# Latent heads' softmax weights turned by VectorE and moved through DRAM, and the ends of the first and last layer reordered

## What is computed

```python
for l in range(DEPTH_2):                       # 2 layers
    h = rmsnorm_2(x, pre_norm_g[l])
    z = h @ w_in[l]
    q_lat, kv_lat, k_pe, gb, gc, xin, q_mem, gate = split_cols(z)
    q = (rmsnorm_2(q_lat, q_norm_g[l]) @ w_uq[l]).reshape(b, s, MLA_HEADS, QK_HEAD_DIM)
    ...
    a_out = mla_attention(q, k, v)             # softmax(q k / sqrt(192)) v, per head
    c_out = short_gated_conv(gb, gc, xin, conv_w[l])
    ...
    m_out = memory_attention(q_mem.reshape(b, s, MEM_HEADS, MEM_HEAD_DIM), mem_n, w_mk[l], w_mv[l])
    y = jnp.concatenate([a_out, c_out, m_out], axis=-1) * jax.nn.silu(gate)
    o = y @ w_o[l]
    x = x + rmsnorm_2(o, post_norm_g[l])
```

## Time and profile before

| | us |
|---|---|
| median of 3 runs | 2250.86 |
| lowest and highest | 2250.55, 2252.74 |
| the profiled execution | 2250.03 |
| its span in the trace | 2248.2 |
| PE busy | 2224.8 (99%) |
| DVE busy | 1309.1 (58%) |
| ACT busy | 808.5 (36%) |

### The profile page before, as it was taken

One profiled execution on the slowest core, in us unless ns is written; L12 is line 12 of the kernel. 1 busy time (PEld: TensorE's weight loads), 2 busy tenths in 40 slices (PEclk: granted clock), 3 DMA queues, 4 the chain that ended last, 5 costly groups with the idle time before them and its releaser, 6 DMA issues.

```text
span 2248.2 us, 27822 instructions
## 1 busy us (share of the span) xinstructions
PE 2224.8 (99%) x10604; PEld 1851.7 (82%) x10604; DVE 1309.1 (58%) x1840; ACT 808.5 (36%) x1264; POOL 115.5 (5%) x151
## 2 busy tenths in 40 slices
PE   8999999999999999999999999999999999999998
PEld 7888888788888888888888888888888888888887
DVE  6677888782248543565556622385434565656565
ACT  6334343443335411343333432244213343335221
POOL 0100010001100100000000011101000000000000
PEclk9999999999999999999999999999999999999999
DMA  7445444453246232212221332373222212122432
GB/s 284 160 152 165 153 155 142 156 165 112 93 172 240 76 113 93 73 64 80 80 72 64 122 103 93 126 267 113 94 93 73 82 61 92 61 81 91 155 116 109
DMA packets 63739, 269.49 MB, mean 120 GB/s; under 512 B 5872, under 2 KB 30704, under 8 KB 40368
## 3 DMA queue, kind: packets, MB, share of 16 engines
q1 hardware_dynamic: 57648, 237.77, 31.9%
q10 hardware_dynamic: 4608, 16.78, 1.9%
q0 software_dynamic: 1408, 13.89, 1.6%
HBM read 236.97 MB, written 31.46 MB: 119 GB/s over the span
## 4 chain that ended last, share of the span: by engine, by line
PE 94%; DVE 3%; ACT 1%; DMA 1%; issue 1%; ACTq 0%; SPq 0%; POOL 0%; DVEq 0%; POOLq 0%
PE acc L497 70%; PE sc L497 10%; PE ov L497 6%; PE sc L845 1%; PE ov L656 1%; DVE lo L1298 1%; ACT hi L951 1%; PE sc L642 1%; PE sc L643 1%; PE sc L837 1%; PE sc L836 1%; DMA g<-xT_dram 0%; DMA raw<-w_dram 0%; PE acc L678 0%; PE acc L679 0%
## 5 line engine op out<-in xcount | busy, mean ns | idle before, releaser
L497 PE MATMUL acc<-h_hi,hi 128*128 128x512 f32 x2240 | 881.1, 393 | 8.1 <-DVE h_lo L1367 7.7
L497 PE MATMUL acc<-h_lo,hi 128*128 128x512 f32 x2240 | 873.5, 390 | 0.0
L497 PE MATMUL acc<-h_hi,lo 128*128 128x512 f32 x2240 | 873.3, 390 | 0.0
L1298 DVE TENSOR_TENSOR lo<-raw,hi 128x2048 fp32r<-128x2048 f32 (+2 forms) x194 | 427.9, 2206 | 392.4 <-ACT hi L951 387.0
L497 PEld LDWEIGHTS acc<-h_hi,hi 128*128 128x128 f32 x2240 | 421.5, 188 | 99.3 <-issue 12.6
L497 PEld LDWEIGHTS acc<-h_hi,lo 128*128 128x128 f32 x2240 | 421.3, 188 | 88.7
L951 ACT ACTIVATE hi<-raw 128x2048 fp32r<-128x2048 f32 (+2 forms) x194 | 358.2, 1846 | 377.8 <-PE acc L497 228.6
L497 PEld LDWEIGHTS acc<-h_lo,hi 128*128 128x128 f32 x2240 | 421.6, 188 | 86.3 <-issue 1.4
L958 ACT ACTIVATE sq<-acc 128x512 f32<-128x512 f32 x32 | 19.2, 600 | 235.8 <-PE acc L497 226.1
L1026 ACT ACTIVATE prob<-prob,st 128x256 f32<-128x256 f32 x128 | 63.6, 499 | 108.6 <-DVE st L1428 108.6
L1819 DVE TENSOR_TENSOR pt_lo<-sc,pt_hi 128x256 fp32r<-128x256 f32 x128 | 43.9, 416 | 47.3 <-ACT pt_hi L1259 47.3
(11 more groups left out here) (286 smaller groups left out, 2881.3 us busy)
## 6 DMA issues: line engine op xcount, KB each, us to landing
raw<-w_dram SPq DMA_DIRECT2D x170, 1024.0 KB, 4.9
turned<-pt SPq DMA_DIRECT2D x32, 448.0 KB, 3.0
pt<-turned SPq DMA_DIRECT2D x64, 224.0 KB, 4.1
xr<-residual ACTq DMA_DIRECT2D x16, 512.0 KB, 5.8
residual<-g ACTq DMA_DIRECT2D x16, 512.0 KB, 5.7
raw<-w_dram SPq DMA_DIRECT2D x8, 896.0 KB, 4.6
raw<-w_dram SPq DMA_DIRECT2D x8, 768.0 KB, 4.2
residual<-g POOLq DMA_DIRECT2D x1, 4096.0 KB, 12.3
```

Of the source, the lines that this page charges most:

```text
L497: ins = pe.matmul(to, a, b, start=first and n == 0, stop=last and n == 2)
L1298: dve.tensor_tensor(lo[c.slot][:, 0:width], raw[c.slot][:, 0:width], hi[c.slot][:, 0:width].bitcast(F32), ALU.subtract).then_inc(lo_done, 1)
```

## The change

- Latent heads: PE no longer turns `prob2`. For each of the four blocks of tokens DVE takes the reciprocal as soon as that block's exponentials are there, scales, and transposes blocks of 32 x 32 into a new buffer `pt2`. SP writes `pt2` to DRAM in two parts (`move_out`) and reads it back in four (`move_in`), in the order that the product needs. ACT makes the high half of it in two parts (`pt_high`), DVE the low half (`pt_low`).
- The values of a head move from behind the next head's projections into its first gate: ahead of tile 9 for the values of an even head, of tile 4 for those of an odd one (`VALUES_AT`). For a layer's last head they go ahead of tile 14 of the output product, in the last layer between two blocks of row products. The low half of the second gate's weights is made earlier.
- First layer's end: the last pair's scores go from tile 8 to 12 of `z_a`, the values of the pair before from ahead of `z_b` to its tile 3, the last values from tile 6 to 11 of the output product. The first pair's scores go from tile 4 to 6.
- `features_behind_y` runs three more tiles of the next chunk ahead of its last tile.
- Memory part: ACT stores only pieces 5 and 6 of the residual in the loop, the other six behind it.
- The last layer's row sums change places in PSUM (banks of `sc` first). Several buffers move.

```diff
+    VALUES_AT, WEIGHTS_AT = (4, 9), (14, 12)
+    STORE_FIRST, STORE_LAST = (5, 6), (4, 7, 0, 1, 2, 3)
...
+            def move_out(no):
+                for n in range(2):
+                    sp.wait_ge(turned2, (no - 1) * TB + (2 * n + 2))
+                    to, src = (x.rearrange("p (a h x) -> p h a x", a=QUADS, h=2)[:, n] for x in (turned2_dram, pt2[:, :]))
+                    sp.dma_start(to, src).then_inc(pt2_out, 16)
+            def move_in(no):
+                sp.wait_ge(pt2_out, no * 32)
+                for keys in range(QUADS):
+                    sp.dma_start(pt2[keys * BLK:(keys + 1) * BLK, :].rearrange("p (a x) -> p a x", a=QUADS),
+                                 turned2_dram.rearrange("(a p) (k x) -> k p a x", a=QUADS, k=QUADS)[keys]).then_inc(pt2_in, 16)
...
-                    for j in range(6):
-                        load2(HEAD + j, i, 6, HW[j // 3] if j % 3 == 0 else CW)
+                    for j in range(2):
+                        no = l * MLA + (i * 2 + (j + 1))
+                        move_out(no)
+                        load2(HEAD + 3 * j + 5, i, 6)
+                        move_in(no)
+                        load2(HEAD + 3 * j + 6, i, 6, HW[j])
+                        load2(HEAD + 3 * j + 7, i, 6)
...
-                         meanwhile=[(4, lambda: scores_first(i))] if first else
+                         meanwhile=[(6, lambda: scores_first(i))] if first else
...
-            features(z_a, h_hi, h_lo, meanwhile=[(8, lambda: scores_first(B))])
-            values_first(A)
-            features(z_b, h_hi, h_lo, last_reader=True)
+            features(z_a, h_hi, h_lo, meanwhile=[(12, lambda: scores_first(B))])
+            features(z_b, h_hi, h_lo, meanwhile=[(3, lambda: values_first(A))], last_reader=True)
...
-                for k in range(KT - lag, KT):
+                for k in range(KT - 1 - lag, KT - 1 - lag + more):
+                    high(d, k, False)
+                pe.wait_ge(y_done, before + KT)
+                k_tile(c, KT - 1, h_hi, h_lo, False, True).then_inc(chunk_done, 1)
+                for k in range(KT - 1 - lag + more, KT):
                     high(d, k, False)
...
-            features_behind_y(0, WO, 0, lambda: values_first(B), 6)
+            features_behind_y(0, WO, 0, lambda: values_first(B), 11)
...
-                def turn_head(no):
-                    pe.wait_ge(probs2, no)
-                    for b in range(TB):
-                        for k in range(TB):
-                            src = b * S + k * P
-                            ins = pe.transpose(bank(b, P, k * P), prob2[:, src:src + P], ident)
-                    ins.then_inc(turned2, 1)
...
                 def values_head(no, i, j):
-                    turned_read(no)
+                    to = ov[0][:, :].rearrange("p (h b a i) -> p a h b i", h=2, b=2, a=QUADS)
                     for k in range(TB):
+                        if k % 2 == 0:
+                            pe.wait_ge(pt2_lo, (no - 1) * 2 + (k // 2 + 1))
...
                     features(chunk2(l, HEAD + 3 * j + 1, i, 6), h_hi, h_lo,
-                             meanwhile=[(2, lambda: turn_mem(MH - 1)), (5, end_of_memory)] if first else [])
+                             meanwhile=[(2, lambda: turn_mem(MH - 1)), (5, end_of_memory)] if first else [(VALUES_AT[j], values_before)])
                     scores_head(no, i, j)
-                    features(chunk2(l, HEAD + 3 * j + 2, i, 6), h_hi, h_lo, meanwhile=[(12, lambda: turn_head(no))], last_reader=last)
+                    features(chunk2(l, HEAD + 3 * j + 2, i, 6), h_hi, h_lo, last_reader=last)
...
+                        if cg == 0 and kg == 1 and b == 1:
+                            values_head(LAYERS * MLA, MLA // 2 - 1, 1)
...
-                        act.dma_start(residual[:, col(l + 1), tile(w, 2 * S)], g[:, tile(w, 2 * S)]).then_inc(stored, 16)
+                        if w in STORE_FIRST:
+                            act.dma_start(residual[:, col(l + 1), tile(w, 2 * S)], g[:, tile(w, 2 * S)]).then_inc(stored_first, 16)
...
+                def pt_high(no):
+                    act.wait_ge(pt2_in, no * (QUADS * 16))
+                    for n in range(2):
+                        act.activation(keys_half(pt_hi, n), keys_half(pt2, n), ACT.Copy).then_inc(pt2_hi, 1)
...
+                def pt_low(no):
+                    for n in range(2):
+                        dve.wait_ge(pt2_hi, (no - 1) * 2 + (n + 1))
+                        dve.tensor_tensor(keys_half(pt2_low, n), keys_half(pt2, n), keys_half(pt_hi, n).bitcast(F32), ALU.subtract)\
+                            .then_inc(pt2_lo, 1)
...
                     for b in range(TB):
-                        pr = prob2[:, tile(b)]
-                        ins = dve.tensor_scalar(pr, pr, rl[:, b:b + 1], None, ALU.mult)
-                    ins.then_inc(probs2, 1)
+                        one, pr = slice(b, b + 1), prob2[:, tile(b)]
+                        if b == 2 and j == 1:
+                            split_next()
+                        dve.wait_ge(exp2, (no - 1) * TB + (b + 1))
+                        link.then(dve.reciprocal(rl[:, one], ls[:, one]))
+                        link.then(dve.tensor_scalar(pr, pr, rl[:, one], None, ALU.mult))
+                        dve.transpose(pt2[:, :].rearrange("p (a h k b i) -> p h b k a i", a=QUADS, h=2, k=TB, b=2)[:, b // 2, b % 2],
+                                      pr.rearrange("p (k a j) -> p k a j", k=TB, a=QUADS)).then_inc(turned2, 1)
+                    if j == 0:
+                        split_next()
```

169 lines of the change are left out of this document (99 added, 70 removed).

## The result

The change made the kernel slower. The median of four runs is 2300.11 us (2299.25 to 2302.9), against 2251.45 us (2250.55 to 2252.74) of the kernel before on the same chip: ratio 1.0219, 95% interval 1.0207 to 1.0232. I had forecast 2233 and a range of 2222 to 2243. The profiled execution has a span of 2297.3 us, 49.1 more than before.

The account below looks back on a forecast made before the run. PE, busy 99% of the span, was taken as the bound; -28.2 + 4.1 + 6.2 + 1.5 + 1.4 - 1.0 - 1.4 = -17.4 us from 2250.0 gave 2233 us, range 2222 to 2243.

Parts of the forecast that it names:

- Turning off PE: Step 1, latent heads: without the 16 PE transposes each of 16 heads saves 1.76 us; strided product taken as free; -28.2 us.
- The new way round: Step 2, each head's path over DVE and DRAM: turned weights arrive in time, 0 us, covers 0.9 (even) and 1.5 (odd).
- the third rival: Transfers through DRAM come late and PE waits before the values; chance 0.14 mild but faster, 0.04 within 0.2%, 0.05 slower.
- G: Reference point in a head: where the second gate's chunk starts on PE; times are counted in us from it.
- E: Reference point in a head: where the second gate's chunk ends on PE, 48 matmuls (10.88 us) after its start.
- x: Microseconds by which each head's turned weights arrive later than forecast; from 2.5 on it eats the whole gain.
- The price per microsecond of lateness: Cost of late transfers as PE waiting in the heads: 8 (x - 0.9) + 6 (x - 1.5); x = 1.5 gives 5 us.
- First gate's wait: Step 3: in 8 odd heads PE waits 0.5 us for the first gate's weights, split late; +4.1 us.
- Layer ends: Step 4, ends of the two last layers: new PE stops, +6.2 us in the first of them, +1.5 us in the last.
- the second rival: The clock falls at the layer ends after closely spaced stops: +1 to +4 us, 2234 to 2237; chance 0.15.
- End of the first layer: Step 5: the stop at 448 goes, but PE waits for y later; +1.4 us, bounds -0.9 and +3.
- Two small ones: Step 6: first pair's scores later removes the stop at 72.17, -1.0 us; fewer residual stores among weight loads, -1.4 us.

Follow-up runs that it names:

- no_trip: Changed kernel without the DRAM writes and reads for the latent heads, blocks not put in order (part of the computation left out): 2240.65 us, ratio 0.9954.
- gains_later: Changed kernel with DVE's wait for the four gain rows moved from ahead of the last layer's third-chunk split to their first reader: 2288.41 us, ratio 1.0171.
- reads_alone: reads_first, with SP also waiting until the four reads have landed before it issues the next weight load: 2266.58 us (one run).
- wide_reads: reads_alone, but each read takes a quarter of the columns to 128 partitions, rows as written (part of the computation left out): 2243.31 us (one run).
- reads_first: Changed kernel with the reads of the turned weights issued ahead of the weight load in the middle heads: 2259.49 us, ratio 1.0032.
- filled: Changed kernel with throwaway 512-column matmuls on PE ahead of each middle head's values, 14 (odd) or 10 (even): 2280.98 us, ratio 1.0141.
- old_stores: The 2232.99 us kernel (transfers covered, gains' wait moved, old first-layer end) with all eight residual pieces stored within the loop again: 2235.40 us, ratio 0.9931.

## Why the prediction was wrong, step by step

The sum again in spans: 2248.2 - 17.4 = 2230.8 forecast, 2297.3 measured. Of the 66.5 us between them, 58.3 are the way through DRAM (no_trip), 6.0 the wait for the gains (gains_later), 1.4 the part up to 730 us; 0.8 are left.

1. **Turning off PE, -28.2: right.** no_trip's pair of heads takes 72.35 us, 72.4 expected, and the strided product costs nothing.
2. **The new way round, 0 us with covers of 0.9 and 1.5: this is the step that failed**, by the third rival's mechanism and far out in its tail. DVE's part was right: all turned at G+8.9 (even) and E+0.0 (odd), put at G+9.0 and E+0.3. The turned weights were in at E+11.0 and E+13.7 instead of E+6.6 and E+8.6: x = 4.4 and 5.1, where I gave x over 2.5 a chance of 0.05. Three errors add up. The writes' leg takes 3.5 us instead of 3.0. For the reads I took 4.1 us behind the last issue from the earlier trace rows, but that is the median of all reads, and the values wait for the *last* of four: 6.0 us in reads_alone, with nothing beside it. Of these 1.9 us nearly all goes with the 32 partitions of each read (wide_reads). Part of it could be read beforehand, too. In the kernel before, the four reads behind 192.72 land after these times, with the last one at 4.9:

```profile
DMA to landing us min/median/max: 3.2/4.1/4.9
```

Third, the load ahead costs 2.0 us (reads_first). The text of step 2 allows up to 1 us for it, and the rival says that a full load ahead is counted, but the times E+6.6 and E+8.6 hold nothing of it: G+9.0 and E+0.3 with the 8.4 us of the transfers give them within 0.1 already. The load right behind costs nothing in the median (7.4 us with and without it). The price per microsecond of lateness was about right for the waiting: 8 (4.4 - 0.9) + 6 (5.1 - 1.5) = 50 us by the formula, and less, 35.6, since DVE is free by then and the even heads' true cover was about 2 us. But the formula had no clock in it. I knew from the earlier trace rows that a stop of 2.34 us is followed by slow matmuls, used that for the layer ends alone, and left it out of the rival with its 14 stops: 19 us (filled).
3. **First gate's wait, +4.1: right.** The stop is 0.26 us, and the first matmul starts 0.64 us behind the one before it instead of 0.23, which with the longer first start makes the 0.5 expected:

```profile
1091.14 0.50 PE L543 MATMUL acc<-h_hi,hi 128*128 128x512 f32 x1 [0.26 <-DVE lo L1364]
```

4. **Layer ends: the first right, the last wrong.** 31.13 us for 31, made of four of the five stops of step 4 (1.0, 2.3, 1.4 and 1.5 there; the fifth, of 0.3, did not come):

```profile
1289.93 0.47 PE L543 MATMUL acc<-h_hi,hi 128*128 128x512 f32 x1 [0.80 <-DVE h_lo L1555]
1295.87 0.50 PE L543 MATMUL acc<-h_hi,hi 128*128 128x512 f32 x1 [2.06 <-DVE h_lo L1555]
1299.23 0.50 PE L543 MATMUL acc<-h_hi,hi 128*128 128x512 f32 x1 [1.03 <-DVE h_lo L1555]
1310.43 0.50 PE L543 MATMUL acc<-h_hi,hi 128*128 128x512 f32 x1 [1.38 <-DVE h_lo L1555]
```

The granted clock in this stretch is 1.00, so the second rival, a slow clock at the layer ends, did not happen here, though a stop of 2.06 us is among them. In the heads a stop of 1.90 us was followed by slow matmuls, so the length of the stop alone does not decide it; what does is not shown. In the last layer I had 1.5 us and it was 7.5. I followed PE's waits for y and missed a chain over three other engines: values later, last high half of y later, POOL's loads of the gains later, DVE's split behind them.

5. **End of the first layer, +1.4: too small.** The stop at 448 is gone and one of 1.98 us stands at 468.06, as forecast. Undoing the edit gave 2.8 us: 1.85 by the end of the output product's first chunks, and 1 behind it, where the next weights' low half stands behind y on DVE. I had ended the step at the matmul of the earlier trace rows and not looked past it.

```profile
468.06 0.47 PE L543 MATMUL acc<-h_hi,hi 128*128 128x512 f32 x1 [1.98 <-DVE h_lo L1555]
...
507.03 0.50 PE L543 MATMUL acc<-h_hi,hi 128*128 128x512 f32 x1 [0.70 <-DVE lo L1364]
```

6. **Two small ones, -1.0 and -1.4:** the stop at 72.17 is gone, and the stop of 1.64 us in the memory part is down to 0.29. Both are right; old_stores has the stores' edit at 2.4 us or more in the covered kernel, where a second stop comes back with them.

With the transfers covered, the gains' wait moved and the first layer's end as before, the kernel takes 2232.99 us. The gain that I forecast for the idea is there; the order of work in the changed kernel does not take it. That this is also the number of the forecast, 2233, is luck: it is another kernel, without the +1.4 of step 5 and with other small terms. The rule on transposes that step 1 quotes from the Trainium skill (VectorE: DVE Perf Modes, Rules for kernel authors) would have been right for the changed kernel, and is not for this one.

## What to carry to other kernels

A time to landing that a page gives as a median over issues is not the time of a transfer made of several: take the last one, into as many partitions as it fills, with the loads ahead of it in the queue. When a wait appears on PE inside a stream of matmuls, price it with the slow clock that can follow, here half of the wait once more. And if an engine in the middle (DVE here) waits for a late transfer, move what is queued behind that wait, not only the work that uses the data.

## What the runs showed of the hardware

- Four reads of 256 KB into 32 partitions each are in 7.4 us after the first issue (median of 12, with nothing beside them), four reads of the same bytes into 128 partitions in 5.6, and one read of the same 1 MB in 4.8.
- A 1 MB load ahead of such reads in the queue put their landing off by 2.0 us, one right behind them by nothing (medians of 12).
- Four reads whose source has 4 as its outermost dimension ran at some 100 GB/s on 0.2 to 0.3 of the DMA engines.
- 164 matmuls more, put in PE's stops, made the kernel 19 us faster, since the granted clock stayed at 1.00.
- Stops of 1.90 us and more ahead of the values were followed by slow matmuls, stops of 1.67 and 1.70 us there and one of 2.06 us at a layer's end were not.
